# A one-core hybrid decoder step: where eight pieces of the gate product stand, and the order of ScalarE's exponents and copies

## What is computed

```python
x = x + 0.5 * swiglu(rms_norm(x, g1), w_gate1, w_up1, w_down1)          # D = 1024, FF = 2816
h = rms_norm(x, g_mix)
q, k, v, iq, ik, iw, hq, hf, hi, hg, ga, gb = split(h @ w_in)
attn = sparse_attention(q, k, v, top-k of the indexer's scores)         # 8 heads x 64, prompt and paged sample
o, s = hgrn2(silu(hq), kf, logf, hi, s0)                                # recurrence, 4 heads of 128 x 128 state
o = rms_norm(o, g_o) * silu(hg)
merged = sigmoid(ga) * (attn @ w_proj_attn) + sigmoid(gb) * (o @ w_proj_hgrn)
x = x + merged @ w_out
x = x + 0.5 * swiglu(rms_norm(x, g2), w_gate2, w_up2, w_down2)
```

## Time and profile before

| | us |
|---|---|
| median of 3 runs | 1691.05 |
| lowest and highest | 1688.89 and 1693.5 |
| the profiled execution | 1692.5 |
| its span, first to last instruction | 1690.7 |
| PE busy | 1619.6 (96%) |
| DVE busy | 735.9 (44%) |
| ACT busy | 452.3 (27%) |
| POOL busy | 696.1 (41%) |

### The profile page before, as it was taken

One profiled execution on the slowest core, in us unless ns is written; L12 is line 12 of the kernel. 1 busy time (PEld: TensorE's weight loads), 2 busy tenths in 40 slices (PEclk: granted clock), 3 DMA queues, 4 the chain that ended last, 5 costly groups with the idle time before them and its releaser, 6 DMA issues.

```text
span 1690.7 us, 29123 instructions
## 1 busy us (share of the span) xinstructions
PE 1619.6 (96%) x12753; PEld 1498.2 (89%) x12753; DVE 735.9 (44%) x1138; ACT 452.3 (27%) x645; POOL 696.1 (41%) x580
## 2 busy tenths in 40 slices
PE   7999999999999999989889889988999999999998
PEld 6999999999976999988867655568999999999998
DVE  6422112224326689974587643345543321023221
ACT  4211112112354224422134333322232211112111
POOL 3443444546431345573542323334443343433432
PEclk9999999999999999997989899999999999999999
DMA  6322334333411232322252388995222322323222
GB/s 166 93 75 60 86 101 117 94 85 111 161 56 40 66 103 75 100 68 84 82 190 71 132 302 338 412 359 218 86 75 76 94 67 73 105 75 95 65 70 91
DMA packets 195230, 203.59 MB, mean 120 GB/s; under 512 B 6416, under 2 KB 181584, under 8 KB 186656
## 3 DMA queue, kind: packets, MB, share of 16 engines
q1 hardware_dynamic: 175344, 107.92, 22.3%
q0 software_dynamic: 12256, 77.93, 12.3%
q10 hardware_dynamic: 7504, 15.88, 2.5%
HBM read 187.21 MB, written 14.30 MB: 119 GB/s over the span
## 4 chain that ended last, share of the span: by engine, by line
PE 88%; DVE 7%; ACT 2%; issue 2%; DMA 1%; POOL 0%; SPq 0%; ACTq 0%; DVEq 0%
PE ps L1696 24%; PE ps L1697 24%; PE ps L1698 24%; PE ps L2167 4%; PE ps L2184 2%; PE ps L2242 1%; DVE att L1385 1%; DVE n_lo L1126 1%; DVE k_lev L1405 1%; PE ps L2075 1%; PE ps L2030 1%; PE ps L1709 1%; DVE prob_p L1467 1%; PE ps L2122 1%; DMA v_more<-in_cache_v,kv_row 1%
## 5 line engine op out<-in xcount | busy, mean ns | idle before, releaser
L528 POOL TENSOR_TENSOR w_lo<-raw,w_hi 128x512 fp32r<-128x512 f32 (+1 forms) x390 | 515.8, 1353 | 707.5 <-ACT w_hi L704 707.5
L1696 PE MATMUL ps<-n_lo,w_hi 128*128 128x288 f32 x1824 | 546.8, 300 | 1.0 <-ACT qT L818 1.0
L1697 PE MATMUL ps<-n_hi,w_lo 128*128 128x288 f32 x1824 | 540.1, 296 | 0.0
L1698 PE MATMUL ps<-n_hi,w_hi 128*128 128x288 f32 x1824 | 538.5, 295 | 0.0
L1696 PEld LDWEIGHTS ps<-n_lo,w_hi 128*128 128x128 f32 x1824 | 344.3, 189 | 11.2 <-issue 10.1
L1698 PEld LDWEIGHTS ps<-n_hi,w_hi 128*128 128x128 f32 x1824 | 345.5, 189 | 0.0
L1697 PEld LDWEIGHTS ps<-n_hi,w_lo 128*128 128x128 f32 x1824 | 344.7, 189 | 0.1
L704 ACT ACTIVATE w_hi<-raw 128x2048 fp32r<-128x2048 f32 (+2 forms) x108 | 188.2, 1742 | 273.3 <-PE ps L1698 271.1
L1697 PE MATMUL ps<-hid_hi,w_lo 128*128 128x288 f32 x704 | 208.4, 296 | 0.0
L1696 PE MATMUL ps<-hid_lo,w_hi 128*128 128x288 f32 x704 | 208.4, 296 | 0.0
L1698 PE MATMUL ps<-hid_hi,w_hi 128*128 128x288 f32 x704 | 208.1, 296 | 0.0
(11 more groups left out here) (305 smaller groups left out, 2246.6 us busy)
## 6 DMA issues: line engine op xcount, KB each, us to landing
raw<-in_ffn_w_gate SPq DMA_DIRECT2D x44, 512.0 KB, 4.0
raw<-in_ffn_w_up SPq DMA_DIRECT2D x44, 512.0 KB, 5.2
raw<-in_ffn_w_down SPq DMA_DIRECT2D x32, 704.0 KB, 4.6
raw<-in_w_in SPq DMA_DIRECT2D x22, 1024.0 KB, 5.3
gates<-scratch_g ACTq DMA_DIRECT2D x4, 1152.0 KB, 10.6
raw<-in_w_out SPq DMA_DIRECT2D x4, 1024.0 KB, 5.0
scratch_x<-xT ACTq DMA_DIRECT2D x1, 2304.0 KB, 12.1
scratch_g<-g_head SPq DMA_DIRECT2D x16, 144.0 KB, 1.8
```

The source lines that it names most:

```text
L528: ins = pool.tensor_tensor(w_lo[:, u % NRAW, part], raw[:, u % NRAW, part], w_hi[:, u % NW, part].bitcast(F32), ALU.subtract)
L1696: pe.matmul(dst, hi, x_lo, start=first, stop=False)
L1697: pe.matmul(dst, lo, x_hi, start=False, stop=False)
L1698: return pe.matmul(dst, hi, x_hi, start=False, stop=last)
```

## The change

The gate product loses its places in the tails. `IN_HEADS` goes from 16 to 8, so that pieces 0 to 3 stand in the levels of g = 0, 4 to 7 in those of g = 1, and 8 to 31 in prompt attention, whose first eight steps (`NARROW`) take two pieces each, the next six one. The pieces of a pair use PSUM banks 5 and 7 in turn; the transposes of the first eight steps share bank 4. On ACT, the exponents of a step stand ahead of the copies of the pieces of the step before. `v_own` is made by two DVE instructions for each g, ahead of the tails' state updates, and no longer by ACT. The top-k search gives one round (two halves) of those in `heads` to prompt attention, which takes up to four halves a step, and the bias work behind it stands one or two steps earlier. POOL's quarters of `w_lo` leave the levels and stand in one piece behind them. Only one quarter of `gates`, not two, is scaled by POOL at the end. The cut diff:

```diff
-    return (3, 2, 0, 1)[n // 2]
+    return (n // 2 + 3) % 4
@@
-        IN_HEADS = 16
+        IN_HEADS = 2 * HB
+        NARROW = HA
+        def pieces_of_step(m):
+            if m < NARROW:
+                return [IN_HEADS + 2 + 2 * m, IN_HEADS + 3 + 2 * m]
+            i = IN_HEADS + 2 + NARROW + m
+            return [i] if i < PIECES else []
+        def gate_bank(i):
+            if i < IN_HEADS:
+                return i % 4
+            if i == IN_HEADS:
+                return 6
+            return 5 if i % 2 == 0 and i < IN_HEADS + 2 + 2 * NARROW else 7
+        def turn_banks(m):
+            return ps[:, 4, :].rearrange("p (e w) -> p e w", e=2) if m < NARROW else ps[:, 4:6, :]
@@ POOL
-                    if 3 <= L <= 6:
-                        low_part(L - 3)
...
-                lows(at_unit["gate", 2 * g + 2 if g == 0 else 4])
+                lows(at_unit["gate", g + 1])
...
-            lows(at_unit["gate", 5])
+            lows(at_unit["gate", 3])
@@ ACT, heads
-                for a in range(2):
-                    own_values(2 * g + a)
-                for i in range(8 * g, 8 * g + 4):
+                for i in range(4 * g, 4 * g + 4):
                     gate_out(i)
...
-                    for i in range(8 * g + 4 + 2 * a, 8 * g + 6 + 2 * a):
-                        gate_out(i)
@@ ACT, prompt attention
-                    if IN_HEADS + 1 + m < PIECES:
-                        gate_out(IN_HEADS + 1 + m)
                     act.wait_ge(S("pp_max"), m + 1)
                     if m:
                         act.wait_ge(S("pp_turned"), m)
...
                     ins.then_inc(S("pp_exp"), 1)
+                    for i in pieces_of_step(m - 1) if m else [IN_HEADS + 1]:
+                        gate_out(i)
                     if m:
                         turned(m - 1)
@@ DVE
-            EARLY = 6
+            EARLY = 5
...
+                    dve.tensor_tensor(v_own[:, a, :, :], v0.unsqueeze(1).to_broadcast([NS, NB, VD]),
+                                      cst[0:NS, C_OWN:C_OWN + NS:NQ].unsqueeze(2).to_broadcast([NS, NB, VD]),
+                                      ALU.mult).then_inc(S("v_own_done"), 1)
...
-                    for _ in range(3):
+                    for _ in range(4):
                         if taken[0] < 2 * ROUNDS:
                             take_half()
@@ PE, gate_piece
-                if part[0] == 0 and not head:
-                    pe.wait_ge(S("gate_out"), i if i > IN_HEADS + 1 else i - 1)
+                if part[0] == 0 and i >= 4:
+                    one = i >= IN_HEADS + 2 + 2 * NARROW
+                    pe.wait_ge(S("gate_out"), i - 3 if i < IN_HEADS else i if one else i - 1)
@@ PE, tails
-                    gate_piece(tail, (0,))
-                    pe.wait_ge(S("k_rows_done"), 2 * g + 2)
+                    pe.wait_ge(S("k_rows_done"), h + 1)
+                    pe.wait_ge(S("gate_out"), 4 * g + 4)
...
-                            gate_piece(*((tail, (1,)), (tail + 1, (0,)), (tail + 1, (1,)))[i - 1])
@@ PE, prompt attention
-                    if IN_HEADS + 2 + m < PIECES:
-                        gate_piece(IN_HEADS + 2 + m, (0, 1))
+                    for i in pieces_of_step(m):
+                        gate_piece(i, (0, 1))
```

More of the change, by code:

```diff
@@ L610, in attention_pages @@
                     value_group(m)
-                for q in (2, 3):
-                    pool.wait_ge(S(f"quarter_in{q}"), X_IN[q] + 16)
-                    for n in range(2):
-                        for a in range(2):
-                            part = gates[:, GATES_AT[q] + n, a, :]
-                            ins = pool.tensor_tensor(part, part, rms[:, :], ALU.mult)
-                    ins.then_inc(S("gate_scaled"), 1)
+                pool.wait_ge(S("quarter_in3"), X_IN[3] + 16)
+                at = GATES_AT[3]
+                for n in range(2):
+                    for a in range(2):
+                        part = gates[:, at + n, a, :]
+                        ins = pool.tensor_tensor(part, part, rms[:, :], ALU.mult)
+                ins.then_inc(S("gate_scaled"), 1)
             def state_load(h):
@@ L916, in gate_out @@
                     split(at_unit["gate", n] + 2)
-            def own_values(h):
-                a, g = h % 2, h // 2
-                if g:
-                    act.wait_ge(S("head_read"), 2 * g)
-                else:
-                    act.wait_ge(S("prompt_biased"), 1)
-                for b in range(NB):
-                    ins = act.activation(v_own[:, a, b, :], stage[0:NS, g, 0, a * VD:(a + 1) * VD], ACT.Copy,
-                                         scale=cst[0:NS, C_OWN + NQ * b:C_OWN + NQ * b + 1])
-                ins.then_inc(S("v_own_done"), 1)
             def heads(g):
-                act.wait_ge(S("stage_done"), NTOK + g + 1)
-                for a in range(2):
-                    own_values(2 * g + a)
-                for i in range(8 * g, 8 * g + 4):
+                for i in range(4 * g, 4 * g + 4):
                     gate_out(i)
@@ L1418, in heads @@
                 for a in range(2):
+                    v0 = stage[0:NS, g, 0, a * VD:(a + 1) * VD]
+                    dve.tensor_tensor(v_own[:, a, :, :], v0.unsqueeze(1).to_broadcast([NS, NB, VD]),
+                                      cst[0:NS, C_OWN:C_OWN + NS:NQ].unsqueeze(2).to_broadcast([NS, NB, VD]),
+                                      ALU.mult).then_inc(S("v_own_done"), 1)
+                for a in range(2):
                     h = 2 * g + a
@@ L2107, in dots @@
                     for e in range(2):
-                        pe.matmul(ps[:, 2 * (m % 2) + e, :width], ident_b[:, :], bias_p[:, at:at + width], start=True, stop=False)
+                        pe.matmul(banks[:, e, :width], ident_b[:, :], bias_p[:, at:at + width], start=True, stop=False)
                     for e in range(2):
                         part = slice(64 * e, 64 * e + 64)
-                        ins = pe.matmul(ps[:, 2 * (m % 2) + e, :width], qT[part, hp, cols(t)], kT[part, hp, NS:NS + width],
+                        ins = pe.matmul(banks[:, e, :width], qT[part, hp, cols(t)], kT[part, hp, NS:NS + width],
                                         start=False, stop=True)
```

91 lines of the change are left out of this document (37 added, 54 removed).

## The result

| | us |
|---|---|
| the kernel before, median of 20 runs | 1690.63 |
| the changed kernel, median of 20 runs | 1699.71 |
| lowest and highest of them | 1690.17 and 1707.49 |
| the forecast | 1714.5 (1700 to 1722) |

The ratio is 1.0048, with a 95% interval of 1.0037 to 1.0060: 8 us slower. The profiled execution of the changed kernel has a span of 1699.0 us, 8.3 more than the one before.

A forecast was written before the change was run, and what follows sets the result against it. PE was taken as the bound. Tails +0.6, levels -1.5, prompt attention steps 0 to 7 +20.4, steps 8 to 13 +2.4, the end +1.5 summed to +23.4 us: median 1714.5 us, range 1700 to 1722.

The follow-up runs named there:

- own_behind_states: The changed kernel with DVE making each head's `v_own` behind that head's four state updates, not ahead of all of them: 1694.04 us.
- copies_and_own: The changed kernel with ACT's gate-piece copies ahead of the exponents again and `v_own` made by ACT again: 1684.57 us, 0.9952 of the kernel before.

## What to carry to other kernels

When filler work is taken out of a recurrence, work out each step as the longest engine's own issue spacing, not as the sum of record lengths round the loop, and look at which engine waits for which. Undo each accompanying edit by itself: here two edits that came with the move (an order on ACT, a product ahead of the first state on DVE) cost 16 us together, and what was left without them gained 8; one of the two was harmless until the filler that covered it left. And where PE is busy with few columns, see whether more columns are free: here they brought 5 to 7 us, in the kernel before too.

## What was not expected of the hardware

- A product with 8 columns and one with 64 take the same time here (16 in 1.95 and 1.90 us), but the first ones leave the granted clock lower over all runs of a kernel (0.982 to 0.986 for 0.987 to 0.991), in the tails themselves or right behind them.
- The time of the changed kernel follows its mean clock closely: among its 20 runs 1690.17 us at 0.988 and 1707.49 at 0.978.
- The same DVE product over 64 x 1024 took 1.21 us with POOL idle and 1.93 beside a burst of POOL, and the burst was longer too: 7.50 us beside these products, 6.54 with them moved away (own_behind_states).
- A half-clock stretch can begin and last while PE is busy throughout (copies_and_own, 820 to 826 us).
